# VectorE makes gated one-hot rows token by token, GpSimd compares for the second key, the loops of the scatter stage are written out

## The reference, cut to what matters

```
scores = jnp.einsum('thcd,hcnd->thcn', q, sub_keys)
sv, si = lax.top_k(scores, PEER_TOPK)
...
idx = jnp.take_along_axis(cand_i, best_p, axis=-1)
gate = jax.nn.softmax(best_s, axis=-1)
...
act = jnp.einsum('td,thkd->thk', xb, u_tab[ib])
wgt = jax.nn.gelu(act) * gb
return jnp.einsum('thk,thkd->td', wgt, v_tab[ib])
```

## Time and profile before

| | us |
|---|---|
| median of 3 runs | 3286.01 (3278.22 to 3293.03) |
| the profiled execution's time | 3282.5 |
| its span in the trace | 3280.7 |

### The profile page before, as it was taken

The page is one execution under the profiler, slowest core; times in us unless marked ns, Lnnn a source line. Parts: engine busy times, 40 slices in busy tenths (PEclk is TensorE's granted clock), DMA queues, the critical chain, the costliest instruction groups (busy, mean ns, idle before and its releaser), DMA issues. The chain is left out here.

```text
span 3280.7 us, 52721 instructions
## 1 busy us (share of the span) xinstructions
PE 3122.7 (95%) x17744; PEld 2695.4 (82%) x17744; DVE 2381.6 (73%) x4997; ACT 1406.0 (43%) x2735; POOL 641.9 (20%) x556
## 2 busy tenths in 40 slices
PE   7899999999999999899989999999999989999999
PEld 5757776777768899888976988988879977988888
DVE  6567776876656686556977777877656788877887
ACT  5454333333346565565264333332564274333332
POOL 0000000000000000155262222222356061222221
PEclk9899999999999999899999999999999999999999
DMA  6115533445323555433518899998334518998996
GB/s 218 42 58 180 173 141 122 141 129 166 95 67 109 159 168 172 142 113 129 176 43 290 316 331 336 334 336 327 129 101 155 167 70 301 338 332 312 338 341 246
DMA packets 176404, 643.35 MB, mean 196 GB/s; under 512 B 20352, under 2 KB 20736, under 8 KB 175360
## 3 DMA queue, kind: packets, MB, share of 16 engines
q1 hardware_dynamic: 138672, 504.62, 45.2%
q0 software_dynamic: 36864, 134.23, 11.4%
q10 hardware_dynamic: 720, 2.71, 0.2%
HBM read 640.44 MB, written 1.05 MB: 196 GB/s over the span
## 5 line engine op out<-in xcount | busy, mean ns | idle before, releaser
L338 ACT ACTIVATE split<-ring 128x512 fp32r<-128x512 f32 (+1 forms) x644 | 397.7, 624 | 699.3 <-PE ps L224 666.7
L224 PE MATMUL ps<-hT,split 128*128 128x512 f32 (+1 forms) x3504 | 630.5, 341 | 6.5 <-DVEq L322 3.5
L224 PEld LDWEIGHTS ps<-hT,split 128*128 128x128 f32 x3504 | 546.1, 191 | 91.1 <-DVE hT L593 9.7
L2696 PE MATMUL ps<-h2F,gates 128*128 128x192 f32 x3200 | 557.5, 328 | 18.1 <-DMA gates<-peer_u 17.9
L2696 PEld LDWEIGHTS ps<-h2F,gates 128*128 128x128 f32 x3200 | 530.9, 191 | 43.9 <-DMA gates<-peer_u 15.2
L347 POOL TENSOR_TENSOR split<-ring,split 128x512 fp32r<-128x512 f32 x184 | 244.6, 1340 | 1529.4 <-ACT split L338 1524.9
L347 DVE TENSOR_TENSOR split<-ring,split 128x512 fp32r<-128x512 f32 (+1 forms) x460 | 307.5, 679 | 283.8 <-ACT split L338 282.9
L2762 ACT ACTIVATE split<-ring 128x512 fp32r<-128x512 f32 x504 | 317.5, 632 | 348.4 <-PE ps L2713 316.2
L2686 POOL DMA_INDIRECT gates<-peer_rows,row_at x256 | 277.0, 1082 | 855.4 <-DVE row_act L2828 471.9
L2821 DVE TENSOR_TENSOR split<-ring,split 128x512 fp32r<-128x512 f32 x504 | 342.7, 691 | 125.5 <-ACT split L2762 125.3
L2755 ACT ACTIVATE gelu<-ps 128x192 f32<-128x192 f32 x200 | 66.2, 331 | 421.3 <-PE ps L2696 421.3
(11 more groups left out here) (389 smaller groups left out, 4753.0 us busy)
## 6 DMA issues: line engine op xcount, KB each, us to landing
ring<-peer_v SPq DMA_DIRECT2D x256, 512.0 KB, 5.6
gates<-peer_u SPq DMA_DIRECT2D x200, 512.0 KB, 6.6
ring<-w_up SPq DMA_DIRECT2D x88, 512.0 KB, 3.7
ring<-w_choose SPq DMA_DIRECT2D x88, 512.0 KB, 3.4
ring<-w_mixing SPq DMA_DIRECT2D x68, 512.0 KB, 3.5
ring<-w_merge SPq DMA_DIRECT2D x64, 512.0 KB, 4.2
ring<-w_down SPq DMA_DIRECT2D x44, 512.0 KB, 3.6
mix_row_ring<-w_mod SPq DMA_DIRECT2D x40, 512.0 KB, 3.7
```

The lines of the kernel that those rows point to most:

```text
L224: ins = nc.tensor.matmul(out, lhsT(a), rhs(b), start=first and n == 0, stop=last and n == len(PASSES) - 1)
L338: self.nc.scalar.activation(self.split[:, self.half_slot(s), 0, cols], self.ring[:, self.slot(s), cols], ACT.Copy).then_inc(self.high_read ...
L2696: last = nc.tensor.matmul(k.ps[:, m % 2, 0:DENSE], k.u_ring[:, m % RAW, c * P:(c + 1) * P], k.h2F[:, c, 0:DENSE], start=c == 0, stop=c == ...
```

## The change

VectorE no longer makes `hot_i` and `hot_j` with two instructions a lot. It makes `hot_i` alone, with one `tensor_scalar` for each token: compare `iota` in PSUM with the slot's key i and multiply with the slot's gate, both given as one value per partition. GpSimd's gating pass is gone. GpSimd now makes `hot_j` of the last three tokens of a lot, one `tensor_scalar` for each, out of the table in SBUF. It waits for `spread` in place of `one_hot`, and TensorE waits for its `key_hot` in place of `gated`. All loops are written out, 48 lots each, so that positions are constants. ScalarE's work and `weigh_early` stay as they were.

```diff
     def lagged(eng, make, keep, lag):
-        for n in range(lots):
-            make(0, n)
+        for n in range(turns_all * lots + lag):
+            if n < turns_all * lots:
+                make(n // lots, n % lots)
             if n >= lag:
-                keep(0, n - lag)
-        with eng.Fori(1, turns_all) as i:
-            for n in range(lots):
-                make(i, n)
-                keep(i + (n - lag) // lots, (n - lag) % lots)
-        for n in range(lots - lag, lots):
-            keep(turns_all - 1, n)
+                keep((n - lag) // lots, (n - lag) % lots)
...
             def one_hots(i, n):
                 dve.wait_ge(spread, i * lots + n + 1)
-                for hot, slot, first in ((k.hot_i, k.slot_i, 0), (k.hot_j, k.slot_j, on_act)):
-                    many = lot - first
-                    keys = slot[:, bass.ds(token(i, n) + first, many)].unsqueeze(2).broadcast_to([P, many, NK])
-                    nc.vector.tensor_tensor(hot[:, n * lot + first:(n + 1) * lot, :], iota[:, 0:many, :], keys,
-                                            ALU.is_equal).then_inc(one_hot, 1)
+                for u in range(lot):
+                    t = bass.ds(token(i, n) + u, 1)
+                    last = nc.vector.tensor_scalar(k.hot_i[:, n * lot + u, :], iota_psum, k.slot_i[:, t], k.slot_gate[:, t], ALU.is_equal, ALU.mult)
+                last.then_inc(one_hot, 1)
...
         @block.gpsimd
         def _(pool):
-            with pool.Fori(0, turns_all) as i:
+            pool.sem_inc(key_hot, lots)
+            for i in range(turns_all):
                 for n in range(lots):
-                    pool.wait_ge(one_hot, (i * lots + n) * 2 + 1)
-                    hot = k.hot_i[:, n * lot:(n + 1) * lot, :]
-                    gates = k.slot_gate[:, bass.ds(token(i, n), lot)].unsqueeze(2).broadcast_to([P, lot, NK])
-                    nc.gpsimd.tensor_tensor(hot, hot, gates, ALU.mult).then_inc(gated, 1)
+                    pool.wait_ge(spread, i * lots + n + 1)
+                    for u in range(on_act, lot):
+                        last = nc.gpsimd.tensor_scalar(k.hot_j[:, n * lot + u, :], k.const("iota"), k.slot_j[:, bass.ds(token(i, n) + u, 1)], None, ALU.is_equal)
+                    last.then_inc(key_hot, 1)
...
-            with pe.Fori(0, turns_all) as i:
+            for i in range(turns_all):
                 for n in range(lots):
                     pe.wait_ge(weighted, i * lots + n + 1)
-                    pe.wait_ge(one_hot, (i * lots + n) * 2 + 2)
+                    pe.wait_ge(one_hot, i * lots + n + 1)
                     pe.wait_ge(act_hot, i * lots + n + 1)
-                    pe.wait_ge(gated, i * lots + n + 1)
+                    pe.wait_ge(key_hot, i * lots + n + 1 + lots)
```

More of the change, by code:

```diff
@@ L2531, in scatter_stage @@
     iota_psum = k.ps[:, 7, 0:NK]
-    iota = iota_psum.unsqueeze(1).broadcast_to([P, lot, NK])
     token = lambda i, n: (i * lots + n) * lot
     def lagged(eng, make, keep, lag):
-        for n in range(lots):
-            make(0, n)
+        for n in range(turns_all * lots + lag):
+            if n < turns_all * lots:
+                make(n // lots, n % lots)
             if n >= lag:
-                keep(0, n - lag)
-        with eng.Fori(1, turns_all) as i:
-            for n in range(lots):
-                make(i, n)
-                keep(i + (n - lag) // lots, (n - lag) % lots)
-        for n in range(lots - lag, lots):
-            keep(turns_all - 1, n)
-    with stage(nc, "one_hot", "gated", "spread", "copied", "weighted", "distance", "act_hot") as (
-            block, one_hot, gated, spread, copied, weighted, distance, act_hot):
+                keep((n - lag) // lots, (n - lag) % lots)
+    with stage(nc, "one_hot", "key_hot", "spread", "copied", "weighted", "distance", "act_hot") as (
+            block, one_hot, key_hot, spread, copied, weighted, distance, act_hot):
         @block.vector
```

## The result

| | median us | range |
|---|---|---|
| before | 3289.52 | 3278.22 to 3310.24 (4 runs) |
| after | 3341.41 | 3332.63 to 3349.61 (4 runs) |

The ratio is 1.0146 with a 95% interval of 1.0108 to 1.0184, so the change costs 36 to 61 us, about 48. The prediction said 3301 and a range up to 3320: the sign came as forecast, the size did not. The profiled execution of the changed kernel took 3349.61 us, with a span of 3347.8.

What follows compares the result with a forecast made beforehand. VectorE was taken to bound the scatter stages, going from 1.28 to 1.50 us a lot. Stages of +9.95 and +8.8 less 2.2 for tails gave +16.5 us, 3301 in all, with an 80% range of 3280 to 3320.

Steps and rivals of the forecast that it cites:

- the sign: Whole kernel: the change makes it slower, by +16.5 us.
- nothing hides a longer stage: Both scatter stages, two of them 4% of the span: a change in their length passes one to one into the total.
- VectorE sets the pace: Scatter stage before the change: VectorE, busy 40.00 of 40.00 us, is the bound at 1.28 us a lot.
- rival (a): Scatter stages: VectorE's per-partition fetches are hidden, step 0.20 us, ScalarE's 1.15 a lot bounds; 3268 or 3271 us, chance 0.17.
- VectorE's term: Scatter lot: four new `tensor_scalar` at 0.33 us a step plus 0.18, so 1.50 us a lot against 1.28.
- The step that failed: Scatter lot on GpSimd: three 128-column comparisons at 0.41 us each, 1.2 a lot, hidden under VectorE's 1.50.
- The sum: Both scatter stages: +9.95 and +8.8 us, less 1.1 each for the tails, +16.5 us in all.
- The tail of 3.4 us: End of each scatter stage, from the last lot's start: 3.4 us in place of 4.46, so -1.1 each.
- (b): Scatter stages: GpSimd becomes the bound at 0.55 us a comparison, 1.65 a lot, +13 on top; 3314 us, chance 0.10.
- (c): Scatter stages: TensorE's granted clock falls, 1.6 to 1.7 us a lot, +13 us; 3314, chance 0.07.

Runs made afterwards that it cites:

- The edit with two comparisons: The changed kernel with GpSimd making two key comparisons a lot in place of three: 3304.39 us, ratio to before 1.0035.
- the other split: Gates put on `hot_j`: VectorE makes plain `hot_i` and one gated row, GpSimd two, ScalarE scales its own; 3321.59 us, ratio to before 1.0084.
- the loops alone: The kernel before with only its four scatter-stage loops written out: 3295.67 us, ratio to before 1.0012.
- the loops with the longer lag: The kernel before with its loops written out and ScalarE's copy lag 2 in place of 1: 3284.22 us, ratio to before 0.9990.

## Why the prediction was wrong

**What bounds the kernel before.** Right that nothing hides a longer stage: the stages' sum follows the measured ratio in every kernel timed in rounds. The edit with two comparisons has 12.5 us more in its stages and a ratio worth 11.5 us (3 to 20), the other split 23.6 and 28 (17 to 38), the changed kernel 42.2 and 48 (36 to 61), the loops alone none and 4 (5 less to 13 more), the loops with the longer lag 5.2 less and 3 less (14 less to 7 more). It was not the whole story that VectorE sets the pace. Next to its 1.24 us a lot lies the round of ScalarE and TensorE, which the lag of 1 makes and which takes 1.275 where the loops are written out. It did not matter for this change, but it decides what rival (a) is worth.

**VectorE's term** was right. Forecast 0.33 a step and 1.50 a lot; measured 0.32 and, with GpSimd out of the way, 1.45. The reading from the earlier trace rows held: a per-partition value adds 0.06 us to the step, and nothing hides it here. The kernels with none, one and two values show 0.20, 0.26 and 0.32. This also bears on the Trainium skill's figure (VectorE: DVE Perf Modes, § The TRN2 errata), 0.26 us for 128 columns without a term for such values. Constants only are recorded at 0.28, so the figure is near there; the instruction of this change is recorded at 0.40, 0.14 more.

**The step that failed** is GpSimd's: "I take 0.41, as a comparison with a per-partition value may cost more than the bare rate: 1.2 us a lot, under VectorE's 1.50, hidden. It decides from 0.50 each." Measured 0.58 each, 1.74 a lot, not hidden. It decided. The mistake has a form. The estimate scaled the pass of 512 columns down with a fixed part of 0.12 us, taken from an instruction of one column. Measured, the fixed part is 0.24 us and a column 2.6 ns, where the estimate had 0.12 and 2.25 ((1274 - 120)/512); no row of before was a small comparison on GpSimd. Both terms were short, by 0.12 and by some 0.05 us. The reason given for the upper figure did not hold: a constant in place of the key left the step at 0.60. Only a second value with its multiply cost more (0.77). The bounds did hold it (up to 1.04), but a chance of 0.10 was too little for a point 0.09 above the value taken when the upper bound lay 0.6 above it. The Trainium skill (GPSIMD Engine Reference, § 4.1 Engine selection) has GpSimd "roughly line-rate" with one input. The runs disagree: 2.6 ns a column against VectorE's 1.08, there out of PSUM.

**The sum.** With 0.58 it closes. 48 lots x 3 x 0.58 = 83.5, plus 0.5 until GpSimd starts and 2.1 from its last comparison to the end of the last early product: 86.1, measured 86.2. Each 0.01 us in that step is worth 2.9 us in the total. The tail of 3.4 us came true where VectorE is the bound: with two comparisons on GpSimd, VectorE's last lot starts at 1739.25 and the stage ends at 1742.68. In the changed kernel VectorE is ahead of GpSimd, and the tail counts from GpSimd's last comparison: 2.1 us, against 2.6 behind GpSimd's last pass before.

**Rivals.** (b) is what happened, and was given a chance of 0.10 and a time of 3314. From there to the measured 3341, 0.58 in place of 0.55 is 8.6 us. Some 4 more come from the sum's shape: it added GpSimd's excess to 43 lots a stage, and left the start to VectorE's pace, where GpSimd sets it from the first lot. Another 5 is the median of before, now 3289.5, where the forecast had 3301 - 16.5 = 3284.5. The last 10 are inside the interval. (a) was wrong even as a rival: with VectorE at 0.20 a step and 0.98 a lot, the stage takes 64.7, the same as before, and not the 57 that ScalarE's 1.15 a lot would give. ScalarE's own time was not the bound there, because ScalarE and TensorE waited for each other in turn; with the lag made 2 the stage fell to 53.1. (c) did not occur, with a clock of 1.00 while TensorE was busy for 25.98 of 40 us.

**What stays open.** Single executions reach the first stage up to 21 us apart with identical code ahead of it, and this goes with the clock granted in the first 600 us: 0.95 to 0.97 in the seven profiles whose stage starts by 1671.3, 0.91 to 0.94 in the six that start later. Over whole executions it is the same: of 17 of the kernel before, the fastest (3271.67 us) had a mean of 0.980 and the slowest (3317.22) 0.966. Why one execution is granted less than another is open. The 6 us between the 42 of the stages and the 48 of the ratio are less than this scatter, and nothing shows that they come from the change.

## What to carry to other kernels

Work that moves to an idle engine needs its price in that engine's own step, with a fixed part measured on that kind of instruction. If the estimate is 20% under the point where it decides, it is not hidden, it is open. Multiply the step by how often it occurs before giving a chance: here 0.01 us was 2.9.

When the busiest engine of a stage is made cheaper, follow the next round of waits and not only the next engine's busy time: who waits for whom, over how many lots, and which lag sets that number.

## What was new about the hardware

- A GpSimd comparison of 128 columns steps by 0.58 us: 0.24 fixed and 2.6 ns a column. A constant in place of the per-partition value shortens its record (674 to 528 ns) and not its step (0.60). A second value with a multiply makes 0.77. The fixed part is from two widths, 64 and 128.
- VectorE's `tensor_scalar` on 128 columns of PSUM steps by 0.20, 0.26 and 0.32 us with no, one and two per-partition values.
- On ScalarE an activation of 128 columns took 0.49 us with a per-partition scale and bias, and 0.31 with constants (the same function both times).
- Identical code took up to 21 us longer to the first scatter stage in executions whose granted clock was lower in the first 600 us (0.91 against 0.95).
